# Weight splits on GpSimd between the key rotations, and the first cached pages inside attention's last units

## The reference, cut to what matters

```python
a = rmsnorm(h, g_attn)
cq, ckv, kr, qs, ks, vs = jnp.split(a @ w_in, SPLIT_POINTS, axis=-1)
q = (rmsnorm(cq, g_qa) @ w_qb)                      # 8 heads x (64 nope + 32 rope)
q_nope = rmsnorm(q[..., :64], g_qn)
q_rope = rope(rmsnorm(q[..., 64:], g_qr), pos)
latent = rmsnorm(ckv, g_kva)
ks = partial_rope(rmsnorm(ks, g_ks), pos)           # window keys, 4 tiles
k_nope, v = decompress(latent)                      # latent @ w_kvb, keys normed by g_kn
# prompt: causal attention in blocks of 128 queries, 8 latent and 8 window heads
# samples: k_nope of 8 x 16 cached pages (128 rows x 256 each) is decompressed only for its norm
```

## Time and profile before

| what | us |
|---|---|
| median of three runs | 1071.72 |
| the three runs | 1070.80, 1071.72, 1075.98 |
| the profiled execution, its own time | 1066.25 |
| its span, first to last instruction | 1064.4 |
| TensorE busy | 1044.6 |
| VectorE busy | 627.7 |
| ScalarE busy | 461.6 |
| GpSimd busy | 108.1 |

### The profile page before, as it was taken

The page is one execution under the profiler, slowest core; times in us unless marked ns, Lnnn a source line. Parts: engine busy times, 40 slices in busy tenths (PEclk is TensorE's granted clock), DMA queues, the critical chain, the costliest instruction groups (busy, mean ns, idle before and its releaser), DMA issues.

```text
span 1064.4 us, 20895 instructions
## 1 busy us (share of the span) xinstructions
PE 1044.6 (98%) x7954; PEld 920.2 (86%) x7954; DVE 627.7 (59%) x1090; ACT 461.6 (43%) x810; POOL 108.1 (10%) x141
## 2 busy tenths in 40 slices
PE   9999999899899999999989999999999999999998
PEld 8998998465677676777759999999999999999998
DVE  5575798876576666766679954434322344434654
ACT  4423433665565655655663443333211222222522
POOL 5322162240000000000001300000000000000000
PEclk9999999999999999999999999999999999999999
DMA  7764813459777677887522364465543545652232
GB/s 274 280 236 155 316 60 112 148 197 341 223 275 237 220 263 254 274 279 242 167 98 69 131 227 169 157 236 197 176 160 133 183 160 175 241 179 99 75 93 90
DMA packets 68591, 202.32 MB, mean 190 GB/s; under 512 B 7425, under 2 KB 40450, under 8 KB 67234
## 3 DMA queue, kind: packets, MB, share of 16 engines
q1 hardware_dynamic: 66338, 131.41, 36.9%
q0 software_dynamic: 2176, 69.90, 18.6%
HBM read 196.20 MB, written 72.13 MB: 252 GB/s over the span
## 4 chain that ended last, share of the span: by engine, by line
PE 90%; DVE 5%; issue 2%; ACT 2%; DMA 0%; POOL 0%; SPq 0%; DVEq 0%; ACTq 0%
PE ps L564 53%; PE ps L1325 17%; PE ps L1423 4%; PE ps L1300 2%; PE ps L1379 1%; PE ps L1341 1%; PE ps L1313 1%; PE ps L1357 1%; PE ps L1373 1%; PE ps L1276 1%; PE ps L1271 1%; PE ps L1345 1%; DVE att L1635 1%; PE ps L1281 1%; PE ps L1178 1%
## 5 line engine op out<-in xcount | busy, mean ns | idle before, releaser
L564 PE MATMUL ps<-aHi,wHi 128*128 128x272 f32 x1152 | 240.8, 290 | 0.2 <-DVE aLo L365 0.2
L564 PE MATMUL ps<-aLo,wHi 128*128 128x272 f32 x1152 | 238.1, 288 | 0.0
L564 PE MATMUL ps<-aHi,wLo 128*128 128x272 f32 x1152 | 236.8, 287 | 0.0
L400 DVE TENSOR_TENSOR wLo<-ring,wHi 128x1024 fp32r<-128x1024 f32 (+3 forms) x102 | 145.0, 1421 | 131.7 <-ACT wHi L395 131.5
L395 ACT ACTIVATE wHi<-ring 128x1024 fp32r<-128x1024 f32 (+3 forms) x102 | 113.4, 1112 | 240.8 <-PE ps L564 214.8
L564 PEld LDWEIGHTS ps<-aHi,wHi 128*128 128x128 f32 x1152 | 180.2, 188 | 2.2 <-issue 1.0
L564 PEld LDWEIGHTS ps<-aLo,wHi 128*128 128x128 f32 x1152 | 181.2, 189 | 0.0
L564 PEld LDWEIGHTS ps<-aHi,wLo 128*128 128x128 f32 x1152 | 180.4, 188 | 0.0
L1674 DVE TENSOR_REDUCE ssq<-att 128x8 f32<-128x512 f32 x128 | 87.1, 680 | 77.1 <-ACT att L964 77.1
L964 ACT ACTIVATE att<-ps 128x512 f32<-128x512 f32 x128 | 76.3, 596 | 100.2 <-PE ps L1325 99.6
L1325 PE MATMUL ps<-wkHi,pgHi 128*128 128x512 f32 x256 | 104.3, 407 | 1.5 <-DVE pgLo L1668 1.2
(11 more groups left out here) (284 smaller groups left out, 1558.4 us busy)
## 6 DMA issues: line engine op xcount, KB each, us to landing
out_o_cv<-in_cv POOLq DMA_DIRECT2D x16, 2044.0 KB, 10.2
ring<-in_wgu SPq DMA_DIRECT2D x44, 512.0 KB, 3.6
big<-in_pgt SPq DMA_DIRECT2D x128, 144.0 KB, 2.8
big<-in_pgl SPq DMA_DIRECT2D x128, 128.0 KB, 2.3
kv<-in_ck SPq DMA_DIRECT2D x8, 1792.0 KB, 10.4
ring<-in_win SPq DMA_DIRECT2D x21, 512.0 KB, 5.2
kv<-in_cv SPq DMA_DIRECT2D x8, 1024.0 KB, 5.5
kv<-in_cv SPq DMA_DIRECT2D x24, 256.0 KB, 5.9
```

The costliest lines, as they stand in the source:

```text
L400: nc.vector.tensor_tensor(wLo[:, u % 2, 0:width], ring[:, u % 2, 0:width], wHi[:, u % 2, 0:width].bitcast(F32), ALU.subtract).then_inc(w_l ...
L564: ins = nc.tensor.matmul(pair[rows, a, 0:HT], w[:, c], xx[:, k, a * HT:(a + 1) * HT], start=(k == 0 and z == 0), stop=(k == nk - 1 and z = ...
```

## The change

Seven edits in one stretch, from input tile 10 to the first cached pages:

1. The low parts of the six query weight tiles are made by GpSimd (`pool_weight`) and not by VectorE: the first behind the closing sum of the third window key tile, the second behind that of the fourth, the others behind that, ahead of the rotary queries.
2. The squares and sums of the prompt keys g_kn stand one step earlier, so that the last sum ahead of the P_KEYS gather is that of a window key tile.
3. The P_QR gather stands in the middle of query tile 3, the P_QN gather behind two values tiles; the other two values tiles stand at units 1 and 3, the last in another PSUM bank.
4. The scalings of the nope queries stand at units 2, 4, 10 and 12; the key weights' low part at unit 18 and not 13.
5. The first three pages are split at units 20 to 23, into buffers of their own in the weight ring (`fstHi`, `fstLo`).
6. The key products of the first two pages stand between the last units' turns of attention, the third behind its last product; the wait for attention's outputs stands after that.
7. The first two output weight tiles are loaded behind the first window values, and not ahead of attention.

```diff
+        def pool_weight(u, width):
+            nc.gpsimd.wait_ge(w_hi, u + 1)
+            nc.gpsimd.wait_ge(w_lo, u)
+            nc.gpsimd.tensor_tensor(wLo[:, u % 2, 0:width], ring[:, u % 2, 0:width], wHi[:, u % 2, 0:width].bitcast(F32),
+                                    ALU.subtract).then_inc(w_lo, 1)
...
-        QN_AT = (2, 5, 7, 9)
+        QN_AT = (2, 4, 10, 12)
...
+        def value_bank(t):
+            return ps[1][:, t % 2, :] if t < 3 else ps[2][:, 1, :]
+
+        FIRST_AT = 20
+
+        def page_parts(g):
+            return (fstHi[:, g, :], fstLo[:, g, :]) if g < AHEAD else (pgHi[:, g % NBUF, :], pgLo[:, g % NBUF, :])
...
-            for u in range(2):
-                sp_weight(W_O + u, wo[u])
...
             load_win_v(0)
+            sp.wait_ge(k_raw, AHEAD)
+            for u in range(2):
+                sp_weight(W_O + u, wo[u])
             sp.wait_ge(w_sc, 1)
             load_win_k(1)
...
                 pool_cos(g)
                 pool_add_cq(2 + i)
                 pool_rope(g)
+                if i >= 2:
+                    pool_weight(W_QB + i - 2, QB_WIDE)
+            for h in range(2, NQT):
+                pool_weight(W_QB + h, QB_WIDE)
             pool_heads(*g_qr)
...
             value_copy(0)
+            value_copy(1)
             head_root(P_QN)
-            value_copy(1)
...
             for n in range(len(units) + LAG_T):
+                if n == len(units) + 1:
+                    page_square(0, 0)
...
                     last.then_inc(a_e, 1)
+                if n - FIRST_AT in range(AHEAD):
+                    page_hi(0, n - FIRST_AT)
...
-                mm3(W_QB + h, P, ps[d % 2], FULL, (cqHi, cqLo), nk=KQ, step=0 if h else 1, parts=cq_lo).then_inc(w_used, 1)
+                mm3(W_QB + h, P, ps[d % 2], FULL, (cqHi, cqLo), nk=KQ, step=0 if h else 1, parts=cq_lo,
+                    mid=(lambda: gather(P_QR)) if h == 3 else None).then_inc(w_used, 1)
...
             for n in range(len(units) + LAG_PV):
+                if len(units) <= n < len(units) + 2:
+                    page_keys(0, n - len(units))
...
                 if n == 0:
                     values_of(0)
+                    values_of(1)
                     gather(P_QN)
-                    values_of(1)
                 if n == 1:
                     values_of(2)
+                if n == 3:
                     values_of(3)
...
+            page_keys(0, 2)
             pe.wait_ge(a_o, H)
             pe.wait_ge(p_nw, 1)
-            pe.wait_ge(wk_lo, 1)
...
-                         12: [(dve_rope, g_qs[2]), (dve_scale, g_qs[3])],
-                         13: [(dve_rope, g_qs[3]), (dve_stat, g_ks[0]), (dve_stat, g_kn[0])],
+                         12: [(dve_rope, g_qs[2]), (dve_scale, g_qs[3]), (dve_stat, g_kn[0])],
+                         13: [(dve_rope, g_qs[3]), (dve_stat, g_ks[0]), (dve_stat, g_kn[1])],
...
-                if d + 2 < NIN + NQT:
-                    dve_weight(d + 2, W_WIDE if d + 2 < NIN else QB_WIDE)
+                if d + 2 < NIN:
+                    dve_weight(d + 2, W_WIDE)
...
             for n in range(len(units) + LAG_PV + 1):
+                if n - FIRST_AT - 1 in range(AHEAD):
+                    page_lo(0, n - FIRST_AT - 1)
...
-                if n == 13:
+                if n == 18:
                     v.wait_ge(wk_hi, 1)
```

More of the change, by code:

```diff
@@ L936, in _ @@
                     value_copy(2)
+                if n == 4:
                     value_copy(3)
@@ L1198, in _ @@
                        12: each((vs_turn, 0), (vs_turn, 1)), 13: each((vs_turn, 2), (vs_turn, 3)), 14: each((vs_turn, 4)),
-                       16: each((gather, P_KEYS)), 23: each((gather, P_QR))}
+                       16: each((gather, P_KEYS))}
             for d in range(NIN + NQT):
@@ L1254, in new_scores, with page_keys @@
                 last.then_inc(p_new, 1)
+            def page_keys(b, t):
+                g = b * NPG + t
+                if g == 0:
+                    pe.wait_ge(wk_lo, 1)
+                    pe.wait_ge(a_sm, 2 * len(units))
+                pe.wait_ge(p_lo, g + 1)
+                hi, lo = page_parts(g)
+                if g >= 2:
+                    pe.wait_ge(k_sq, g - 1)
+                for c in range(KC):
+                    for z, (x_, w_) in enumerate(((hi, wkHi), (hi, wkLo), (lo, wkHi))):
+                        last = mm(ps[0][:, g % 2, :], x_[:, c * P:(c + 1) * P], w_[:, c, :],
+                                  start=(c == 0 and z == 0), stop=(c == KC - 1 and z == 2))
+                last.then_inc(k_raw, 1)
             for n in range(len(units) + LAG_PV):
+                if len(units) <= n < len(units) + 2:
+                    page_keys(0, n - len(units))
                 if n == ABSORB:
@@ L1731, in _ @@
             dve_tail = {3: row_max, 5: probs, 8: recip, 12: turned_out}
-            for t in range(AHEAD):
-                page_lo(0, t)
             for b in range(NB):
```

91 lines of the change are left out of this document (48 added, 43 removed).

## The result

The changed kernel took 1078.58 us in the median of 8 runs (1075.75 to 1082.66), the kernel before 1071.8 in 8 runs beside it. The ratio is 1.0066, 95% interval 1.0047 to 1.0084: some 7 us slower. The profiled execution took 1077.41 us with a span of 1075.6, against 1066.25 and 1064.4 for the kernel before. That trace of the kernel before is a quick one: its 92 timed runs in this case took 1067.13 to 1075.98, so times read against the trace make the change look dearer than the medians do.

What follows compares the result with a forecast made beforehand. TensorE, busy 98% of the span at full clock, bounds the kernel; only its waits count. Terms 6.9 - 0.4 - 0.6 - 1.4 - 0.5 = +4.0 us on the median of 1071.72 gave 1075.7, range 1069 to 1080.

Steps and rivals of the forecast that it cites:

- the side that had 0.23: Chance given to a result slower by over 0.5%: the falling-clock rival and a fifth of the forecast.
- Gathers, -1.0: Before and inside the query tiles: TensorE's waits at the first two gathers, 0.39 and 0.62 us, go.
- Low parts, +6.9: Query tiles: GpSimd's low parts come late for tiles 0 and 1; tile 1 begins at 161.75 instead of 154.85.
- The waits of 3.8 and 3.1 us: Query tiles: TensorE's forecast waits for GpSimd's low parts ahead of tile 0 and tile 1.
- all three turns that the prediction counts: Query tiles: VectorE's scaling, rotation product and scaling (0.79, 0.72, 0.79 us) each go between GpSimd operations.
- rival (a): Query tiles: GpSimd seldom loses its turn, so low parts cost +4.6, +1.7 in all, 1073.4 us; chance 0.20.
- The +4.6: Query tiles: cost of the low parts if GpSimd never loses a turn to VectorE, instead of +6.9.
- Attention, -1.4: Attention units: old waits and the third gather go, 4.4 us; new waits of 3.0 come; between 0 and -3.0.
- the four waits foreseen: Attention: new TensorE waits of about 1.0 at unit 3, 0.5 at 6, 1.2 at 11, 0.3 at 13.
- Handover, -0.5: From attention to cached pages: 1.9 us won by page 4, then a 1.4 wait for window keys; 0 to -1.9.
- the charge for the keys: Handover, page 12: window keys land at 298.3, no sooner than before; TensorE asks at 296.9 and waits 1.4 us.
- Rival (c), the clock: Query tiles: TensorE's clock falls after the new waits, tiles take 9.06 instead of 4.53; +9.9 us, 1081.6; chance 0.12.

Runs made afterwards that it cites:

- e3_low_vector: The changed kernel with the low parts of all six query weight tiles back on VectorE; 1072.65 us, ratio 1.0020 to the kernel before.
- e10_late_four: e9_vector_copies with the low parts of query weight tiles 2 to 5 on GpSimd again, 0 and 1 on VectorE; 1065.9 us, ratio 0.9959 to the kernel before.
- e1_scale_back: The changed kernel with the four nope query scalings back at units 2, 5, 7 and 9; 1071.98 us, ratio 1.0004 to the kernel before.
- e2_keys_first: The changed kernel with element 0's window keys issued by SyncE ahead of its sixteen latent pages; 1072.82 us, ratio 1.0012 to the kernel before.
- e5_copies_early: The changed kernel with GpSimd's first four window-cache copies ahead of the decode-query layout; 1069.68 us, ratio 0.9984 to the kernel before.
- e9_vector_copies: The changed kernel with low parts on VectorE and the first four window-cache copies ahead of the layout; 1065.28 us, ratio 0.9954 to the kernel before.
- e7_late_scale_before: The kernel before with only the last two nope query scalings moved from units 7 and 9 to 10 and 12; 1074.78 us, ratio 1.0034 to it.
- e6_copies_held: The changed kernel with the last four window-cache copies held until element 0's window keys landed; 1091.92 us, ratio 1.0196 to the kernel before.

## Why the prediction was right or wrong

The forecast was 1075.7 in a range of 1069 to 1080, within 0.5% as the likeliest; it came to 1078.58, within the range, and at 0.66% slower on the side that had 0.23. Two terms were wrong in opposite directions, so the nearness of the sum says little for its working.

- **Gathers, -1.0.** Right. The waits of 0.39 and 0.62 are gone. In e3_low_vector, which keeps these edits and not the low parts, the first unit comes 1.5 us sooner than in the kernel before, 0.4 of it by the end of the input tiles (149.63 against 150.06), where the first gather stands, and 1.1 inside the query tiles, where the second does; other edits lie in these stretches too, so the parts are not shown one by one.
- **Low parts, +6.9.** The place was right (two low parts between rotations, none behind; e10_late_four) and so were the turns, but the term was mis-sized: 4.7 to 4.9 us by the runs, 4.8 in the trace of the changed kernel. The waits of 3.8 and 3.1 us came to 2.52 and 0.41, the second shorter by 1.8 because tile 0 itself took longer at the lower clock. GpSimd did give way at all three turns that the prediction counts, but each turn cost it 0.41 to 0.47 us (2.26 where a low part alone takes 1.85, 1.83 and 1.80 where the operation alone takes 1.36), not 0.72 to 0.79: 1.3 us and not 2.3. The rotation closed at 150.38 and not at 151.4, another 1.0; low parts of 1.83 to 1.85 instead of 1.92 and operations without a gap make the rest. So the price of rival (a) came out without its condition, that GpSimd seldom loses its turn, and in part by luck: in e1_scale_back and e2_keys_first the same rotation closed 1.9 and 2.0 us behind the input tiles' end and not 0.2, TensorE waited 4.25 and 4.29 us at tile 0, and the low parts cost 7.1 and 6.6. The Trainium skill, "SBUF — State Buffer", "Who interferes with whom", says that whoever issues first has the shared pair of ports for the whole instruction and the other is fully blocked; it says so of VectorE's two-port modes, and of two-input operations that they contend. In e10_late_four this is seen in full: a small VectorE operation (L518, 0.18 us in the changed kernel) took 1.77, from 161.01 to 162.78, beside GpSimd's low part that ended at 162.75. The +4.6 that the prediction drew from the rule by letting GpSimd keep every turn came nearer in size, but the trace does not show that it kept them.
- **Attention, -1.4.** Right in size. From the first unit's scores to the last unit's latent scores it took 92.21 us before and 90.99 in the changed kernel, -1.2; of the four waits foreseen, 1.0, 0.5, 1.2 and 0.3, the trace has 1.02, 0.46, 1.12 and 0.37.
- **Handover, -0.5.** Half right. From there to the first element's scores: 34.72 us before, 33.01 in e5_copies_early, where no key is late: 1.7 won, 1.9 foreseen. But the charge for the keys was a wait of 1.4, and the wait came to 5.66; with the clock behind it the keys cost 8.05 us in the traces and 8.8 by the ratios (the changed kernel against e5_copies_early). **This is the step that failed.** It said that SyncE's string "does not come sooner"; I took that for "comes as before". In the paragraph on attention I moved the memsets of the layout to unit 12 along with the last scaling, and did not move what stands behind them on the same queue; of GpSimd's queue I wrote that nothing else on it is urgent. The eight copies are not urgent, but their transfers are in the way of something that is. The trace of the kernel before shows how little it took: the DMA share fell to 0.21 at 274 to 278 us, just when SyncE issues.
- **Rival (c), the clock.** It came in part and elsewhere. In the query tiles of the changed kernel the granted clock fell to 0.85 and 0.81 and cost next to nothing, since tile 1 waited for GpSimd anyway; no kernel took the 9.9 us in this stretch. At the late keys it cost about 2.4 us: the span of units is 132.27, less 5.66 of wait, less 124.22 of e5_copies_early.

By the terms as measured: +4.8 for the low parts, +8.8 for the keys, and for all other edits what e9_vector_copies shows without both, -4.9 (0.9954); the sum is +8.7, the runs gave +7.1. The 1.6 between lie within the intervals of the terms (about 2 us to either side) and are not explained further; e3_low_vector and e7_late_scale_before, the other kernels with a wait for the keys, also ran 1 and 3 us faster than the columns of the table make them (first unit and span of units against the kernel before: +3.1 and +6.9; by the ratio +2.1 and +3.6), so the wait may be shorter in other executions than in the profiled ones, or the kernel before may lose more in executions other than its profiled one; no trace tells which. The forecast's gains without the keys (-0.4, -0.6, -1.4, -1.9, together -4.3) were close to those 4.9.

The profiled pair differs by 11.2 us, the medians by 6.8: the profiled execution of the kernel before lies 5.5 below its median, that of the changed kernel 1.2 below, so "none" in the first row of the table is shown for that one execution. Of the 11.2, 2.3 lie behind the first element's scores, in code that is the same; 1.5 of that is a fall of the clock to 0.66 at 559 to 564 us in the changed kernel, which the kernel before did not have there. Other runs vary as much in that stretch, so it is not put to the change.

## What to carry to other kernels

When a step moves, move on paper everything that stands behind it on the same queue, the transfers that nobody waits for above all, and look at the DMA share where they then fall. A mean over the span says little here: GpSimd, busy 10% of it, had no gap at the two operations that counted, so ask for the load of that stretch. And put bulk copies ahead of a wait that they don't need, where the DMA engines are idle.

## What the runs showed of the hardware

- **An issue can stand.** SyncE's five page issues took 4.73 us where the DMA share beside them was 0.09 to 0.45, 6.29 where copies were just ending, and 10.59 to 11.80 where it was 0.86 to 1.18 in the 8 us from 274 to 282 (the changed kernel and e7_late_scale_before). A single issue took 0.34 us undisturbed, up to 6.15 in the changed kernel, and 14.61 behind the four copies of e6_copies_held. The Trainium skill, "DMA: Bandwidth & Descriptors", "Issuing engines are not separate DMA queues", says that transfers of all issuing engines run on the same 16 DMA engines and interleave, and calls the time of an issue usually small beside the transfer. The first agrees with the shares, in which copies of GpSimd and loads of SyncE stand together. The second holds for the undisturbed 0.34 us and not under the copies: there one issue alone stood for 6.15 us, while the five pages, counted from their issue, landed after 3.3 us in the median. What exactly the issue waits for, no run shows.
- **Landing times follow.** The same 1,792 KB took 7.3 to 9.7 us from issue to landing at the handover, 36.7 in e6_copies_held, 14.6 of it in the issue.
- **The clock after a wait.** After waits of 5.5 and 5.66 us for the keys TensorE ran at the lower of its two levels for some microseconds (granted clock 0.50, scores of 3.2 instead of 1.72 us); after the 2.01 us wait in e1_scale_back it fell as well (0.51 at 220 to 225), after the same 2.02 us in the kernel before it did not.
- **VectorE waits out a GpSimd operation.** Beside GpSimd's low part of 1.84 us a VectorE operation of 0.18 us took 1.77 (e10_late_four); in the changed kernel two-input operations of 0.72 to 0.79 us took 1.10 to 1.50 and each ended some 0.55 us after GpSimd's, which in turn were stretched by 0.41 to 0.47.
